# A mixture of experts on TensorE: blocks of 32 tokens on four column groups instead of 64 on two

## What is computed

```python
xb = xt[toks]                                  # rows of one expert's tokens, 1024 wide
h = jax.nn.silu(xb @ w1[e]) * (xb @ w3[e])     # w1, w3: 1024 x 512
return (h @ w2[e]) * gts[:, None]              # w2: 512 x 1024
```

## Time and profile before

| what | value |
|---|---|
| median of 3 runs | 1198.32 us (1197.93 to 1200.55) |
| profiled execution: first to last instruction | 1197.2 us |
| expert stage in it | about 640 to 1161 us |
| PE, DVE, ACT, POOL busy | 91%, 43%, 33%, 16% of the span |
| DMA | 308.9 MB, 258 GB/s over the span, about 420 GB/s from 690 to 1110 us |
| blocks, experts | 41, 32 |

### The profile page before, as it was taken

The page is one execution under the profiler, slowest core; times in us unless marked ns, Lnnn a source line. Parts: engine busy times, 40 slices in busy tenths (PEclk is TensorE's granted clock), DMA queues, the critical chain, the costliest instruction groups (busy, mean ns, idle before and its releaser), DMA issues.

```text
span 1197.2 us, 15506 instructions
## 1 busy us (share of the span) xinstructions
PE 1093.9 (91%) x5142; PEld 659.8 (55%) x5142; DVE 520.2 (43%) x893; ACT 400.4 (33%) x629; POOL 190.7 (16%) x236
## 2 busy tenths in 40 slices
PE   5999999999999999999968999999998898999960
PEld 4888888888866667878854333333332333333320
DVE  5741512111038897463363535352443343341518
ACT  5421323222135665112214242424143324233232
POOL 0110011010100000000001323232323333231210
PEclk9999999999999999999987999999998999998985
DMA  8733331711350005557368899999999999999536
GB/s 305 282 122 116 114 123 44 292 57 45 139 210 12 1 1 176 176 192 306 123 270 353 353 421 420 419 420 419 421 415 420 421 420 420 419 420 419 218 157 258
DMA packets 69248, 308.89 MB, mean 258 GB/s; under 512 B 9024, under 2 KB 9152, under 8 KB 43872
## 3 DMA queue, kind: packets, MB, share of 16 engines
q1 hardware_dynamic: 56144, 273.86, 57.4%
q0 software_dynamic: 13072, 34.63, 7.5%
HBM read 278.57 MB, written 39.06 MB: 265 GB/s over the span
## 4 chain that ended last, share of the span: by engine, by line
PE 69%; DMA 15%; DVE 9%; ACT 3%; issue 3%; SPq 0%; DVEq 0%; ACTq 0%; POOLq 0%; POOL 0%
PE ps L872 18%; PE ps L584 13%; PE ps L585 13%; PE ps L586 13%; DMA rawe<-in_w 11%; PE ps L899 7%; DMA x_scratch<-x 2%; PE ps L862 1%; DVE cur13b L1671 1%; ACT prob L1003 1%; PE ps L881 1%; DVE att L1376 1%; DVE mx L1356 1%; DVE mx L1355 1%; DMA ya<-y_scratch 1%
## 5 line engine op out<-in xcount | busy, mean ns | idle before, releaser
L584 PE MATMUL ps<-whi,xTh 128*128 128x512 f32 x480 | 187.8, 391 | 14.0 <-DVE wlo L1231 14.0
L585 PE MATMUL ps<-wlo,xTh 128*128 128x512 f32 x480 | 187.5, 391 | 0.0
L586 PE MATMUL ps<-whi,xTl 128*128 128x512 f32 x480 | 187.4, 391 | 0.0
L872 PE MATMUL ps<-cur13a,xT 128*64 128x512 f32 x656 | 159.3, 630 | 2.0 <-DVE xT L1648 1.6
L1671 DVE COPY cur13a<-rawe 128x4096 f32 x31 | 71.1, 2294 | 189.1 <-DMA rawe<-in_w 119.7
L872 PE MATMUL ps<-cur13b,xT 128*64 128x512 f32 x656 | 147.8, 592 | 0.0
L899 PE MATMUL ps<-cur,hT 128*64 128x512 f32 x640 | 146.2, 598 | 0.0
L1200 ACT ACTIVATE cur<-rawe 128x4096 f32 x31 | 112.1, 3617 | 3.7 <-issue 1.4
L969 ACT ACTIVATE zst<-ps,rstd 128x512 f32<-128x512 f32 x60 | 40.8, 687 | 204.4 <-PE ps L586 198.0
L584 PEld LDWEIGHTS ps<-whi,xTh 128*128 128x128 f32 x480 | 90.6, 189 | 33.0 <-issue 14.0
L585 PEld LDWEIGHTS ps<-wlo,xTh 128*128 128x128 f32 x480 | 90.7, 189 | 18.8
(11 more groups left out here) (212 smaller groups left out, 1384.1 us busy)
## 6 DMA issues: line engine op xcount, KB each, us to landing
rawe<-in_w SPq DMA_DIRECT2D x96, 2048.0 KB, 25.9
raw<-in_w_in SPq DMA_DIRECT2D x20, 1024.0 KB, 8.0
z_scratch<-zst POOLq DMA_DIRECT2D x60, 256.0 KB, 2.3
gat<-z_scratch SPq DMA_DIRECT2D x12, 512.0 KB, 3.9
xn_scratch<-rrow POOLq DMA_DIRECT2D x6, 1024.0 KB, 5.6
ya<-y_scratch SPq DMA_DIRECT2D x6, 1024.0 KB, 10.8
raw<-in_w_out SPq DMA_DIRECT2D x4, 1024.0 KB, 6.8
xcol<-in_x_cols SPq DMA_DIRECT2D x6, 512.0 KB, 10.2
```

The source lines that it names most:

```text
L584: pe.matmul(out, ah, bh, start=first, stop=False)
L585: pe.matmul(out, ah, bl, start=False, stop=False)
L586: return pe.matmul(out, al, bh, start=False, stop=last)
L872: mm = pe.matmul(ps[0][u * CAP:(u + 1) * CAP, :], xT[:, c, h * CAP:(h + 1) * CAP], cur13[h][:, :, c * 512 + u * 256:c * 512 + u * 256 + 25 ...
```

## The change

`CAP` becomes 32. A block has up to 32 tokens, partition p holds quarter p // 32 of the token in slot p % 32 (256 channels), and a gathered or stored row is 1 KB instead of 2. On the reference's inputs there are 62 blocks instead of 41. `up` and `down` address the array as four column groups of 32, each with a quarter of the output columns, so a matmul has 256 moving columns instead of 512 and there are twice as many per block. There is one transpose instead of two for the hidden values and two instead of four for the rows.

Besides: `xg` and `ystage` have two buffers each with a semaphore each, loops take pairs of blocks, and POOL prepares a store's index before it waits for the result. w1 and w3 are laid out so that a partition's 16 KB are one row of DRAM instead of two of 8 KB; w2 comes in rows of 4 KB instead of 8. The normed rows are written with their channels reordered to match (`rrow`). On DVE, `next_up` does `xT` and the hidden values first and then both weight copies, which no longer wait for the halves of `up` singly. The diff, cut to that:

```diff
-CAP = 64
-MAXB = T // CAP
-NOV = (2 * T) // (CAP + 1)
-NB = NE + NOV
+CAP = 32
+NQ = P // CAP
+QW = D // NQ
+NOV = (2 * T - 3) // CAP
+NB = (NE + NOV + 1) // 2 * 2
...
-        e_w = [A[n][0].rearrange("e (h p c) f -> e p h (c f)", h=2, p=P) for n in ("w1", "w3", "w2")]
+        e_w = [A[n][0].rearrange("e (p h c) f -> e p h (c f)", h=2, p=P) for n in ("w1", "w3")]
+        e_w.append(A["w2"][0].rearrange("e (c p) n -> e p c n", p=P))
...
-                sp.dma_start(rawe[:, c:c + 2 * PIECE].rearrange("p (h n) -> p h n", h=2),
+                sp.dma_start(rawe[:, c:c + 2 * PIECE].rearrange("p (h n) -> p h n", h=2 if k < 2 else 4),
...
+            def rows_to_columns(b, k, n):
+
+                pe.wait_ge(s_gx[k], 16 * n + 16)
+                for c in range(2):
+                    mm = pe.transpose(ps[2][:, c * P:(c + 1) * P], xg[k][:, c * P:(c + 1) * P], ident)
                 mm.then_inc(s_tx, 1)
...
-                        for u in range(2):
-                            mm = pe.matmul(ps[0][u * CAP:(u + 1) * CAP, :], xT[:, c, h * CAP:(h + 1) * CAP],
-                                           cur13[h][:, :, c * 512 + u * 256:c * 512 + u * 256 + 256],
+                        x = (2 * h + c // 2) * CAP
+                        for u in range(NQ):
+                            mm = pe.matmul(ps[0][u * CAP:(u + 1) * CAP, 0:256], xT[:, c % 2, x:x + CAP],
+                                           cur13[h][:, :, c * 512 + u * P:c * 512 + (u + 1) * P],
                                            start=(h == 0 and c == 0), stop=(h == 1 and c == 3))
                     mm.then_inc((s_13a, s_13)[h], 1)
...
-                for k in range(2):
-                    mm = pe.transpose(ps[1][:, k * P:(k + 1) * P], hh[:, k::2], ident)
-                mm.then_inc(s_hT, 1)
+                pe.transpose(ps[1][:, 0:P], hh[:, :], ident).then_inc(s_hT, 1)
...
-                for h in range(2):
-                    for k in range(2):
-                        for u in range(2):
-                            c = h * PIECE + k * D + u * 512
-                            w2 = rawe[:, LAST_W2 + c:LAST_W2 + c + 512] if last else cur2[:, c:c + 512]
-                            mm = pe.matmul(ps[6][u * CAP:(u + 1) * CAP, :], hT[:, k, h * CAP:(h + 1) * CAP],
-                                           w2, start=(h == 0 and k == 0), stop=(h == 1 and k == 1))
+                for k in range(4):
+                    for u in range(NQ):
+                        c = k * D + u * QW
+                        w2 = rawe[:, LAST_W2 + c:LAST_W2 + c + QW] if last else cur2[:, c:c + QW]
+                        mm = pe.matmul(ps[6][u * CAP:(u + 1) * CAP, 0:QW], hT[:, k * CAP:(k + 1) * CAP],
+                                       w2, start=(k == 0), stop=(k == 3))
...
+            with pe.Fori(1, pairs) as j:
+                for k in range(2):
+                    b = 2 * j - 1 + k
+                    up(b)
+                    rows_to_columns(b + 1, k, j)
+                    down(b - 1)
+                    hidden_to_columns(b)
+            last = pe.value_load(nbi[0:1, 1:2], min_val=NE // 2 - 1, max_val=NB // 2 - 1)
+            up(2 * last + 1)
+            down(2 * last)
+            hidden_to_columns(2 * last + 1)
+            down(2 * last + 1, last=True)
...
-                dve.scalar_tensor_tensor(out=rrow[t % 2][:, :], in0=x2[t % 3][:, :], scalar=rstd[:, t:t + 1],
-                                         in1=g2[:, :], op0=ALU.mult, op1=ALU.mult).then_inc(s_rr, 1)
+                dve.scalar_tensor_tensor(out=rrow[t % 2][:, :].rearrange("p (c k) -> p c k", c=KC),
+                                         in0=x2[t % 3][:, :].rearrange("p (k c) -> p c k", c=KC),
+                                         scalar=rstd[:, t:t + 1],
+                                         in1=g2[:, :].rearrange("p (k c) -> p c k", c=KC),
+                                         op0=ALU.mult, op1=ALU.mult).then_inc(s_rr, 1)
...
 
                 e, e1 = expert_of(dve, b), expert_of(dve, b + 1)
+                columns_of_rows(b + 1)
+                hidden(b)
                 with dve.If(e1 > e):
 
...
                     pair = rawe[:, bass.ds((e1 % RING) * EW, 4 * PIECE)].rearrange("p (k n) -> p k n", k=2)
                     dve.wait_ge(s_c13, 2 * e1)
                     for h in range(2):
-                        dve.wait_ge((s_13a, s_13)[h], b + 1)
                         dve.tensor_copy(cur13[h][:, :, :], pair[:, :, h * PIECE:(h + 1) * PIECE]).then_inc(s_c13, 1)
-                columns_of_rows(b + 1)
-                hidden(b)
...
+            def next_gather(j, k):
+
+                pool.wait_ge(s_gx[k], 16 * j)
+                pool.tensor_copy(idxb[:, k:k + 1], idxt[:, bass.ds(2 * j + k, 1)]).then_inc(s_ic, 1)
+                pool.wait_ge(s_tx, 2 * j - 1 + k)
+                pool.wait_ge(s_ic, 2 * j - 1 + k)
+                pool.sem_inc(s_idx, 1)
+                gather(k, idxb[:, k:k + 1])
+
+            def store(j, k):
+
+                if not isinstance(j, int):
+                    pool.wait_ge(s_ys[k], 16 * j)
+                pool.tensor_copy(idxs[:, k:k + 1], idxt[:, bass.ds(2 * j + k, 1)]).then_inc(s_is, 1)
+                pool.wait_ge(s_yc, 2 * j + k + 2)
+                pool.wait_ge(s_is, 2 * j + k + 2)
                 pool.sem_inc(s_ids, 1)
...
```

More of the change, by code:

```diff
@@ L93, in constants @@
     put("iota", np.arange(P))
-    put("half", 4 * CODES + (i // CAP)[:, None])
+    put("half", 8 * CODES + (i // CAP)[:, None])
     put("tok", i[:, None])
@@ L225, in hybrid_layer @@
     cur2 = at("cur2", F_O + 16 * KB, [P, 2 * PIECE])
[L226 to L231, removed]
+    xT = at("xT", F_O + 32 * KB, [P, 2, P])
+    xg = [at(f"xg{k}", F_O + (33 + k) * KB, [P, QW]) for k in range(2)]
+    ystage = [at("ystage0", F_O + 35 * KB, [P, QW]), at("ystage1", F_O + 36 * KB, [P, QW])]
+    hT = at("hT", REL_O, [P, P])
+    sg = at("sg", REL_O + 1 * KB, [P, P])
+    hh = at("hh", REL_O + 2 * KB, [P, P])
     ya = [at(f"ya{t}", RAW_O + t * 8 * KB, [P, 2, D]) for t in range(NT)]
@@ L344, in hybrid_layer @@
         s_gc = sem("s_gc")
-        s_gx = sem("s_gx")
+        s_gx = [sem(f"s_gx{k}") for k in range(2)]
         s_idx = sem("s_idx")
@@ L357, in hybrid_layer @@
         s_yc = sem("s_yc")
-        s_ys = sem("s_ys")
+        s_ys = [sem(f"s_ys{k}") for k in range(2)]
         s_md = sem("s_md")
@@ L855, in _ @@
             pe.wait_ge(s_nb, 1)
[L856 to L862, removed]
+            pairs = pe.value_load(nbi[0:1, 0:1], min_val=NE // 2, max_val=NB // 2)
+            def rows_to_columns(b, k, n):
+                pe.wait_ge(s_gx[k], 16 * n + 16)
+                for c in range(2):
+                    mm = pe.transpose(ps[2][:, c * P:(c + 1) * P], xg[k][:, c * P:(c + 1) * P], ident)
                 mm.then_inc(s_tx, 1)
@@ L1203, in step @@
                 act.sem_inc(s_gc, 1)
[L1204 to L1208, removed]
+            step(1, 0)
+            step(2, 1)
+            step(3, 0, 1)
+            with act.Fori(2, pairs) as j:
+                step(2 * j, 1, j - 1)
+                step(2 * j + 1, 0, j)
+            last = act.value_load(nbi[0:1, 1:2], min_val=NE // 2 - 1, max_val=NB // 2 - 1)
+            rows_out(2 * last + 1, 1, last)
             for t in range(NT):
@@ L1625, in _ @@
                 one_hot(q)
-            dve.tensor_scalar(nbi[:, 1:2], ends[0:1, NE - 1:NE], 1.0 / CAP, -1.0, ALU.mult, ALU.add)
-            dve.tensor_scalar(nbi[:, 0:1], ends[0:1, NE - 1:NE], 1.0 / CAP, None, ALU.mult)
+            for k in range(3):
+                n = dve.tensor_scalar(nbu[:, k:k + 1], ends[0:1, NE - 1:NE], 1.0 / CAP, float(1 - 2 * k), ALU.mult, ALU.add)
+            link(n)
+            dve.tensor_scalar(nbi[:, :], nbu[:, :], 1, None, ALU.logical_shift_right)
             dve.wait_ge(s_br, 1)
-            dve.tensor_copy(served[:, :], ps[5][0:1, 0:NB + 1])
+            dve.tensor_copy(served[:, :], ps[5][0:1, 0:NB])
             dve.wait_ge(s_tbm, 2 * NT)
-            dve.tensor_scalar(idxt[:, :], ps[4][:, 0:NB + 1], -2.0, C("half"), ALU.mult, ALU.add).then_inc(s_nb, 1)
+            dve.tensor_scalar(idxt[:, :], ps[4][:, 0:NB], -4.0, C("half"), ALU.mult, ALU.add).then_inc(s_nb, 1)
             dve.wait_ge(s_re, 3)
@@ L1681, in _ @@
             columns_of_rows(0)
-            with dve.Fori(0, nb - 1) as b:
-                next_up(b)
-            hidden(nb - 1)
+            with dve.Fori(0, pairs - 1) as j:
+                next_up(2 * j)
+                next_up(2 * j + 1)
+            last = dve.value_load(nbi[0:1, 1:2], min_val=NE // 2 - 1, max_val=NB // 2 - 1)
+            next_up(2 * last)
+            hidden(2 * last + 1)
             def last_norm(a, b):
@@ L1742, in _ @@
             pool.sem_inc(s_is, 1)
-            pool.memset(xg[:, :], 0.0).then_inc(s_zr, 1)
-            pool.wait_ge(s_zr, 1)
+            for k in range(2):
+                pool.memset(xg[k][:, :], 0.0).then_inc(s_zr, 1)
+            pool.wait_ge(s_zr, 2)
```

(30 more changed lines are left out.)

100 lines of the change are left out of this document (39 added, 61 removed).

## The result

| | before | changed |
|---|---|---|
| median | 1199.38 us (1197.93 to 1200.55, 4 runs) | 1208.16 us (1205.79 to 1211.52, 4 runs) |
| ratio | | 1.0077, 95% interval 1.0058 to 1.0095 |
| span of the profiled execution | 1197.2 us | 1203.7 us |
| last store issued | 1159.04 | 1166.34 |

The changed kernel is slower by 0.8%. The forecast was 1195.0 with 1187.0 to 1208.0. In the profiled executions the difference is 6.5 us, and the last store is 7.3 later, so it arises before that store.

A forecast was written before the change was run, and what follows sets the result against it. It took DMA to bound the landing of w3(28), and PE and ACT the tail behind it. Landing -0.8 and tail -2.5 made -3.3: span 1193.9, median 1195.0 us, range 1187.0 to 1208.0.

The forecast's parts named there:

- The block: PE's time for one block of 32 tokens: 6.04 us instead of 11.72, with four column groups running beside each other.
- slow issue: Rival, 12%: PE's matmuls issue more slowly than they stream; 1200.3 at 62 ns a record, 1208 at 70 ns.
- groups that take turns: Rival, 6%: column groups on PE don't run four at a time; a block takes 11.2 us, the kernel about 1385.
- The landing: When w3 of expert 28 arrives by DMA: five terms, together 0.8 us earlier.
- The dip at 680: DMA rate drop while SP's queue waits for ScalarE's w2 copy; shorter blocks remove it: -4.5 us, at least -2.
- the other four terms: DMA costs: w2 rows +2.5 us, w1 and w3 rows -2.3, gathers and stores +3.0, the start +0.5.
- the term of +3.0: Gathers and stores in rows of 1 KB instead of 2 cost DMA time: +3.0 us ahead of the last landing.
- The weights' own terms: DMA row sizes: w2 in rows of 4 KB +2.5 us, w1 and w3 in rows of 16 KB -2.3.
- The term for the start: Larger `Bt` on DVE and the strided write of the normed rows: +0.5 us, 0 to 2.
- So PE becomes slack between experts; only the landing and the tail count.: Expert stage: 62 blocks of 6.04 make 374 us of PE, while weights keep landing from 640 to about 1126.
- The tail: From the landing of w3(28) to the last store: 83.8 us against 86.3, so -2.5.
- The clock falls at each switch: Rival, 8%: each PE idle of 2 to 2.5 us costs 1.8 again for a cold `up`, 5.4 in all: 1200.4.

The follow-up runs named there:

- the kernel with the parted copies: Changed kernel, VectorE's first weight copy put ahead of xT and the hidden values, the second left behind them: 1186.44 us, ratio 0.9896 to the kernel before.
- the run with the old order: Changed kernel with VectorE's earlier order, both weight copies ahead of xT and the hidden values: 1193.83 us, ratio 0.9961 to the kernel before.

## Why the prediction was wrong

**The block: right.** `up`, rows, `down` and hidden values were put at 3.58, 0.34, 1.86 and 0.26, 6.04 in all; in the middle of expert 28 one block follows another in 6.08 (1102.23, 1108.31). Four groups do run beside each other: the 32 records of a half of `up` take 1.75, 0.219 a set of four, 55 ns a record. So the rivals of slow issue and of groups that take turns fall. The Trainium skill's figure with hardware decode off ("TensorE: Matmul & The Clock Gate", section "Wait — 56ns, not 53.3ns?"), about 62 ns a matmul, does not bound here: the trace shows 55 a record, and two records, 109 ns, for each of the kernel's 16 matmuls of a half. Which decode was on no run shows.

**The landing: right in kind, and too pessimistic.** w3(28) was put 0.8 earlier and came 5.1 earlier (3.2 in the kernel with the parted copies). The dip at 680 is gone, as forecast:

```profile
678.00:680.00 2.00, 1.63 (x29) 0.68 (x20) 1.25 (x3) 0.48 (x2) 1.62 (x2) 1.00 0.94 389
680.00:682.00 2.00, 0.29 (x8) 0.26 (x12) 2.00 (x2) 1.78 (x2) 1.54 (x1) 1.00 1.00 403
682.00:684.00 2.00, 2.00 (x32) 1.32 (x28) 1.70 (x1) 1.92 (x1) 1.58 (x1) 0.65 1.04 406
```

389, 403 and 406 GB/s instead of 178, 56 and 82. Over 640 to 700 the rate is 407 GB/s instead of 373, 4.9 us of transfer won where 4.5 was put. From 700 to 1060 it is 418 instead of 419, 0.9 us lost, where the other four terms had put 3.7 lost in all. What was mis-sized is the price of smaller rows, above all that of the gathers and stores. The queues in 700 to 1060, before and then in the changed kernel (packets, MB, share of 16 engines):

```profile
q1 hardware_dynamic: 18409, 142.01, 94.9%
q0 software_dynamic: 4640, 8.94, 6.5%
```

```profile
q1 hardware_dynamic: 18269, 141.77, 95.0%
q0 software_dynamic: 4128, 8.76, 6.4%
```

Queue 0, gathers and stores, moves 8.94 MB in 6.5% before and 8.76 MB in 6.4% now: 382 and 380 GB/s, so rows of 1 KB cost what rows of 2 KB cost; the term of +3.0 was nothing. The packet counts fit that: there are not more of them but fewer, and by the trace's records over 95% of the bytes go in packets of 4096 in both kernels (2154 and 2060 of them), so a row, of either size, does not go as a packet of its own. The weights' own terms go against each other. On queue 1 a packet of 8192 bytes took 314.7 ns on the mean before; now 4096 take 163.4 and 16384 take 619.9. For 29 experts that is an estimate of +5.6 for w2, put at +2.5, and of -4.4 for w1 and w3, put at -2.3. The term for the start was not tried. Why the landing of the changed kernel is another 2 earlier than with the parted copies was not tried either; with the same loads it lies between 1067.6 and 1071.3 in five of the kernels here.

**The step that failed: "So PE becomes slack between experts; only the landing and the tail count."** It set 62 x 6.04 = 374 us against the weights, and left out what the next part put on every change of expert. The tail charged three switches with 1.9 to 2.55 of idling each and 0.5 for the second half; the other 28 were charged with nothing. They have the same price, since VectorE does the same work there. By the text's own numbers: 31 x (1.9 to 2.55, and 0.5) = 74 to 95, and some 15 waits for ScalarE of 1.3, 20: 374 + 74 + 20 = 468 to 489 against about 480 of weights. That is no slack, and the sum on one line would have shown it. The trace has 76.6 for those waits, 2.5 each. PE's chain is the bound from expert 13 on, and `up` of expert 28 starts at 1081.32, 13.7 behind its weights, where 2.9 were forecast: 10.8 us.

**The clock: a rival that was put in too few places.** "The clock falls at each switch" had 8% and a price for three switches. It falls at most of the 31: the first `up` of an expert takes 5.0 to 6.4 in 23 of them and 4.0 in the other 8. In 1071.4 to 1074.4, behind 2.31 of idling, the granted clock (the number ahead of the DMA share and the GB/s) is 0.56 of full speed, so nearly all of it at 1.2 GHz, the lower of its two levels; in 1102.2 to 1105.8, an `up` in the middle of expert 28, it is 1.00:

```profile
1071.40:1074.40 3.00, 3.00 (x32) 1.91 (x36) 1.97 (x1) 2.17 (x2) 2.31 (x2) 0.56 1.03 429
1102.20:1105.80 3.60, 3.60 (x65) 1.98 (x64) 0.00 (x0) 0.67 (x3) 1.31 (x3) 1.00 1.02 428
```

Over the stage that is 282.7 - 62 x 3.84 = 45 us of PE's path, over half of the idling itself, and with it the 468 to 489 become 513 to 534; from the first `up` to the end of the last `down` PE takes 520. That price was not tried by itself; it is read from the same work at either pace, and the run with the old order, which keeps pauses of 2 us and has fewer cold `up`s, points the same way.

**The tail: right but for that clock.** From `up` of expert 28 to the last store were forecast 83.8 - 2.9 = 80.9; it took 85.0. Ten periods 60.8 (60.4); idling at three switches 2.09, 2.85, 2.84 = 7.8 (7.0, as the branch takes 0.73 and not 0.45); waits for ScalarE 3.4 (3.9); cold halves of `up`, and halves held up by their copy, 6.4 (3.3, with one cold `up` where there were three); no rows behind the last block -0.3, as put; from the hidden values to the store 6.6, as put. The last is plain to see:

```profile
1160.32 1.45 PEld L900 LDWEIGHTS ps<-rawe,hT 128*32 128x32 f32 x32 [0.68 <-ACT hT L1182]
...
1160.50 3.62 ACT L1208 ACTIVATE cur<-rawe 128x4096 f32 x1 [0.23 <-issue]
...
1165.07 0.38 ACT L1189 ACTIVATE ystage<-ps 128x256 f32<-128x256 f32 x1 [0.95 <-ACT cur L1208]
1166.34 0.98 POOL L1790 DMA_INDIRECT y_scratch<-ystage,idxs  x1 [4.18 <-ACT ystage L1189]
```

The last `down` runs at 1160.32; its results wait for ScalarE's copy of a w2 that nobody reads, 3.62 long.

Together: landing -4.3 against the forecast, PE's lateness +10.8, tail +4.1, 10.6 more than the 1155.7 for the store that the forecast implies; 1166.34 was measured.

**What was right by accident.** 1195 is nearly what the kernel with the old order takes, 1193.8. That the two numbers are close is luck: the run with the old order has cold `up`s and waits that the forecast did not count, and an earlier landing that it did not count either. The change does hold a gain, in the short blocks and their second buffers, and a loss of 14 to 22 that the forecast had seen and priced in the tail alone.

## What to carry to other kernels

When a change shortens a block, list again what stood in the block's shade: work per expert does not shrink with the block, and its place in a queue, harmless in 11.7 us, costs in 6.1. A price found for the tail is to be multiplied by the number of times it is paid, before a resource is called slack, and a pause of PE is to be priced with the slower pace that can follow it, as it did at 23 of 31 changes here. A large copy that is needed by halves can be parted around the small urgent work: here that is worth 1.8% of the whole.

## What the runs showed of the hardware that was not expected

GpSimd's small work stretches while VectorE copies 4096 columns. In the changed kernel at 1114 (timeline; the gather's issue is 1.03 elsewhere):

```profile
1114.06 2.29 DVE L1688 COPY cur13a<-rawe 128x4096 f32 x1 [0.73 <-issue]
...
1114.34 4.34 POOL L1769 DMA_INDIRECT xg<-xn_scratch,idxb  x1 [0.85 <-issue]
...
1116.27 2.29 DVE L1688 COPY cur13b<-rawe 128x4096 f32 x1
...
1118.67 0.20 POOL L1786 COPY idxs<-idxt 128x1 int32 x1
```

It starts in the first copy and ends 0.1 after the second. Of the 62 stores of the changed kernel 29 are issued while one of these copies runs, and take 2396 ns on the mean; the other 33 take 1030, and none of them over 1044. The issues of stores over the stage, in the changed kernel and before:

```profile
L1790 POOL DMA_INDIRECT y_scratch<-ystage,idxs x62 | 103.5, 1669 | 96.5 <-ACT ystage L1189 67.4 <-POOL idxs L1786 17.4 <-issue 10.0
```

```profile
L1767 POOL DMA_INDIRECT y_scratch<-ystage,idxs x41 | 42.3, 1033 | 37.6 <-POOL idxs L1764 35.3 <-issue 2.3
```

1669 ns instead of 1033 on the mean, since the copies now fall into the time of the stores; with the parted copies it is 1225. What holds them up was not tried. None of it was on PE's path here: with two buffers, no transpose waited for rows but for the first.
